# Mixers' second half reordered with other PSUM banks, and upward products with both halves of the activations in one moving operand

## The reference, cut to what matters

```
for l in range(2):
    h = rmsnorm(x, norm_mix_g[l])
    uv, z, xbc, dt_raw, c_q, c_kv, k_rope = split_cols(h @ w_in[l])
    y_a = gmlp_mixer(uv, ...)        # gelu, spatial gate: u * (W_s v + b)
    y_b = ssd_mixer(z, xbc, ...)     # state space mixer
    y_c = mla_mixer(c_q, c_kv, ...)  # 6 heads of causal attention, chunks of 128
    x = x + concat(y_a, y_b, y_c) @ w_out[l]
    x = x + square(relu(rmsnorm(x, norm_mlp_g[l]) @ w1)) @ w2     # 1024 -> 4096 -> 1024
return rmsnorm(x, final_norm_g)
```

## Time and profile before

| | |
|---|---|
| median of 3 runs | 1304.95 us (1301.78 to 1305.06; all: 1304.95, 1305.06, 1301.78) |
| profiled execution | 1302.27 us, span 1300.5 us, mean granted clock 0.998 |
| PE busy | 1258.7 us (97%), 8024 matmuls |
| DVE busy | 870.8 us (67%) |
| ACT busy | 705.1 us (54%) |
| mixers and feed-forward part, layer d0 | about 690 to 818 us and 818 to 997 us of the span |
| the same, layer d1 | about 1000 to 1114 us and 1114 to 1293 us |

### The profile page before, as it was taken

One profiled execution on the slowest core, in us unless ns is written; L12 is line 12 of the kernel. 1 busy time (PEld: TensorE's weight loads), 2 busy tenths in 40 slices (PEclk: granted clock), 3 DMA queues, 4 the chain that ended last, 5 costly groups with the idle time before them and its releaser, 6 DMA issues.

```text
span 1300.5 us, 20111 instructions
## 1 busy us (share of the span) xinstructions
PE 1258.7 (97%) x8024; PEld 1100.9 (85%) x8024; DVE 870.8 (67%) x1570; ACT 705.1 (54%) x1029; POOL 2.4 (0%) x8
## 2 busy tenths in 40 slices
PE   8999999999999999999999999999999999999996
PEld 7997787878888787877998987999998987999895
DVE  6677996684664756548557997655547897665545
ACT  5634577454467666575536675634444576544442
POOL 0000000000000000000000000000000000000000
PEclk9999999999999999999999999999999999999999
DMA  9454532444643335233353544465655544456660
GB/s 273 148 170 136 162 115 81 162 162 162 209 148 130 128 105 170 84 130 106 114 168 100 176 140 132 160 196 181 207 163 150 150 162 119 148 188 193 195 210 33
DMA packets 147058, 197.28 MB, mean 152 GB/s; under 512 B 4732, under 2 KB 102294, under 8 KB 146966
## 3 DMA queue, kind: packets, MB, share of 16 engines
q1 hardware_dynamic: 146838, 195.96, 47.0%
q0 software_dynamic: 128, 0.04, 0.0%
HBM read 194.94 MB, written 1.05 MB: 151 GB/s over the span
## 4 chain that ended last, share of the span: by engine, by line
PE 78%; DVE 12%; ACT 5%; issue 4%; SPq 1%; DMA 0%; DVEq 0%; ACTq 0%
PE bank L481 22%; PE bank L483 22%; PE bank L482 22%; PE bank L569 4%; DVE w_lo L2144 3%; DVE stat L2164 2%; PE bank L1064 1%; PE bank L778 1%; PE bank L682 1%; PE bank L1101 1%; ACT w_hi L1578 1%; DVE stat L2161 1%; DVE arena L2158 1%; PE bank L926 1%; DVE stat L2158 1%
## 5 line engine op out<-in xcount | busy, mean ns | idle before, releaser
L2144 DVE TENSOR_TENSOR w_lo<-w_raw,w_hi 128x2048 fp32r<-128x2048 f32 (+5 forms) x190 | 413.8, 2183 | 139.2 <-ACT w_hi L1578 136.9
L1578 ACT ACTIVATE w_hi<-w_raw 128x2048 fp32r<-128x2048 f32 (+5 forms) x190 | 346.2, 1828 | 282.6 <-PE bank L483 273.1
L481 PE MATMUL bank<-h_hi,w_hi 128*128 128x256 f32 x976 | 279.2, 286 | 4.3 <-DVE w_lo L2144 2.4
L482 PE MATMUL bank<-h_lo,w_hi 128*128 128x256 f32 x976 | 276.1, 283 | 0.0
L483 PE MATMUL bank<-h_hi,w_lo 128*128 128x256 f32 x976 | 276.0, 283 | 0.0
L481 PE MATMUL bank<-w_hi,r_hi 128*128 128x512 f32 (+3 forms) x536 | 207.3, 387 | 3.9 <-DVE r_lo L2843 2.0
L482 PE MATMUL bank<-w_lo,r_hi 128*128 128x512 f32 (+3 forms) x536 | 204.1, 381 | 0.0
L483 PE MATMUL bank<-w_hi,r_lo 128*128 128x512 f32 (+3 forms) x536 | 204.1, 381 | 0.0
L481 PEld LDWEIGHTS bank<-h_hi,w_hi 128*128 128x128 f32 x976 | 187.0, 192 | 12.0 <-issue 9.3
L482 PEld LDWEIGHTS bank<-h_lo,w_hi 128*128 128x128 f32 x976 | 187.1, 192 | 0.5
L483 PEld LDWEIGHTS bank<-h_hi,w_lo 128*128 128x128 f32 x976 | 187.0, 192 | 0.0
(11 more groups left out here) (301 smaller groups left out, 1368.9 us busy)
## 6 DMA issues: line engine op xcount, KB each, us to landing
w_raw<-in_mlp_w SPq DMA_DIRECT2D x64, 1024.0 KB, 5.4
w_raw<-in_w_out SPq DMA_DIRECT2D x24, 1024.0 KB, 5.1
w_raw<-in_w_in_c SPq DMA_DIRECT2D x48, 512.0 KB, 4.6
w_raw<-in_w_in_c SPq DMA_DIRECT2D x18, 1024.0 KB, 5.1
w_raw<-in_w_in_a SPq DMA_DIRECT2D x12, 1024.0 KB, 7.4
w_raw<-in_w_in_b SPq DMA_DIRECT2D x12, 1024.0 KB, 5.1
w_raw<-in_w_in SPq DMA_DIRECT2D x8, 1024.0 KB, 5.2
w_raw<-in_w_out SPq DMA_DIRECT2D x8, 512.0 KB, 3.7
```

Source lines behind the costliest of these rows:

```text
L481: nc.tensor.matmul(o, lhs[0], rhs[0], start=start, stop=False)
L482: nc.tensor.matmul(o, lhs[0], rhs[1], start=False, stop=False)
L1578: nc.scalar.activation(w_hi[:, u % SPLIT_SLOTS, 0:kts * n], w_raw[:, u % RAW_SLOTS, 0:kts * n], ACT.Copy).then_inc(w_rounded.sem, w_rounde ...
L2144: v.tensor_tensor(w_lo[:, s, 0:m], w_raw[:, u % RAW_SLOTS, 0:m], w_hi[:, s, 0:m].bitcast(F32), ALU.subtract)\
```

## The change

Mixers' second half:
- KT_BANK goes from (3, 0, 3) to (3, 0, 0), HEAD_BANK from (3, 6) to (4, 6), and the six heads' scores from the banks 4, 5, 4, 5, 4, 5 to 4, 5, 6, 3, 4, 5.
- PE: turn_mixer comes before turn_heads(2).
- ACT: head_tiles(2) comes after the mixer's high parts; the rounding for ("uv", 1), which is that of the unit mix_out(0, 1), goes from ahead of pair_exp(1) to behind pair_turned(1); that for ("t", 3), the unit mix_out(1, 1), from ahead of the "co" 0 copy to behind pair_turned(2).
- DVE: pair_max(0) comes after spatial_norm and the mixer's low parts; pair_max(2) before pair_normal(1); the split of the unit mix_out(1, 0), weights(("uv", 1), 2), after pair_normal(1).

Feed-forward part, upward products:
- h_hi and h_lo become two halves of one tensor h_both, and the eight banks one tensor.
- For each tile m and k-tile, one matmul with w_hi stationary takes [h_hi | h_lo], 512 columns, into a whole bank, and one with w_lo stationary takes h_hi, 256 columns, into the bank's first half. A unit uses two banks, 2u and 2u + 1.
- ACT copies the second halves of both banks to SBUF (in place of Relu). DVE adds them to the first halves, then computes max(f, 0) * f in one instruction. ACT copies that into r_hi (in place of Square), DVE subtracts as before.

```diff
-        QT_BANK, KT_BANK, ... HEAD_BANK, ... = (7, 6, 7), (3, 0, 3), 7, (1, 2), (3, 6), (6, 7)
+        QT_BANK, KT_BANK, ... HEAD_BANK, ... = (7, 6, 7), (3, 0, 0), 7, (1, 2), (4, 6), (6, 7)
+        MLA_SCORE_BANK = (4, 5, 6, 3, 4, 5)
...
                 turn_heads(1)
+                turn_mixer()
                 turn_heads(2)
-                turn_mixer()
                 scores(1)
...
                 def up(e):
                     for u in range(2):
-                        feature_major((L, "up", e, u), (2 * e + u) % 4, ...)
+                        key = (L, "up", e, u)
+                        for m in range(2):
+                            if 2 * u + m in left:
+                                pe.wait_ge(*left[2 * u + m])
+                            left[2 * u + m] = up_summed.after(key)
...
+                            for m in range(2):
+                                o = bank[2 * u + m]
+                                for k in range(k0, k0 + step):
+                                    hi, lo = [a[:, k, m * P:(m + 1) * P] for a in w]
+                                    nc.tensor.matmul(o, hi, h_both[:, :, k, :], start=k == 0, stop=False)
+                                    i = nc.tensor.matmul(o[:, 0:S], lo, h_hi[:, k, :], start=False, stop=k == KT - 1)
...
                 head_tiles(1)
-                head_tiles(2)
                 act.wait_ge(product_done.sem, product_done.at((L, "bt", 0)))
...
+                head_tiles(2)
                 pair_exp(0)
...
-                round_weights((L, "uv", 1))
                 pair_exp(1)
                 pair_turned(0)
                 pair_exp(2)
                 pair_turned(1)
-                round_weights((L, "t", 3))
+                round_weights((L, "uv", 1))
...
                 pair_turned(2)
+                round_weights((L, "t", 3))
...
-                        nc.scalar.activation(relu, bank[t][:, :], ACT.Relu).then_inc(act_read.sem, act_read.next((L, "up", e, u)))
+                        nc.scalar.activation(low, up_sums(e, u, 1), ACT.Copy).then_inc(up_low.sem, up_low.next(key))
...
+                        act.wait_ge(up_square.sem, up_square.at(key))
-                        nc.scalar.activation(flat2(r_hi[:, t0:t0 + 2, :]), relu, ACT.Square)...
+                        nc.scalar.activation(flat2(r_hi[:, t0:t0 + 2, :]), split_t[:, u, :], ACT.Copy)...
...
                 mixer_norm()
-                pair_max(0)
                 spatial_norm()
...
+                pair_max(0)
                 spatial_gate()
                 pair_max(1)
                 split_lo((L, "at"), ...)
                 pair_normal(0)
+                pair_max(2)
+                pair_normal(1)
                 weights((L, "uv", 1), 2)
-                pair_normal(1)
-                pair_max(2)
                 pair_normal(2)
...
-                        tt(f, relu, relu, MUL)
+                        v.tensor_tensor(f..., up_sums(e, u, 0), low..., ADD).then_inc(up_summed.sem, up_summed.next(key))
+                        dve.wait_ge(up_summed.sem, up_summed.at(key))
+                        v.scalar_tensor_tensor(f, f, 0.0, f, ALU.max, MUL).then_inc(up_square.sem, up_square.next(key))
```

More of the change, by code:

```diff
@@ L160, in build @@
         w_lo = sb("w_lo", [P, SPLIT_SLOTS, UNIT], F32R)
-        h_hi = sb("h_hi", [P, KT, S], F32R)
-        h_lo = sb("h_lo", [P, KT, S], F32R)
+        h_both = sb("h_both", [P, 2, KT, S], F32R)
+        h_hi, h_lo = h_both[:, 0, :, :], h_both[:, 1, :, :]
         r_hi = sb("r_hi", [P, YT, S], F32R)
@@ L183, in build, with up_sums @@
         arena = sb("arena", [P, ARENA])
-        bank = [ctx.enter_context(nc.psum_tensor(f"bank{i}", [P, 512], F32)) for i in range(8)]
+        banks_all = ctx.enter_context(nc.psum_tensor("bank", [P, 8, 512], F32))
+        bank = [banks_all[:, i, :] for i in range(8)]
+        def up_sums(e, u, part):
+            at = 2 * u
+            return banks_all[:, at:at + 2, part * S:(part + 1) * S]
         def K(name):
@@ L253, in build @@
         square_hi = Steps("square_hi")
+        up_low = Steps("up_low")
+        up_summed = Steps("up_summed")
+        up_square = Steps("up_square")
         latent_normal = Steps("latent_normal")
@@ L388, in build @@
         XS_BANK, CB_BANK, WST_BANK, UV_BANK, ST_BANK, YD_BANK, YO_BANK = (4, 5), 0, 6, (1, 2), 4, (5, 0), 4
-        QT_BANK, KT_BANK, GATING_BANK, MIXER_BANK, HEAD_BANK, MLA_TURN_BANK = (7, 6, 7), (3, 0, 3), 7, (1, 2), (3, 6), (6, 7)
+        QT_BANK, KT_BANK, GATING_BANK, MIXER_BANK, HEAD_BANK, MLA_TURN_BANK = (7, 6, 7), (3, 0, 0), 7, (1, 2), (4, 6), (6, 7)
+        MLA_SCORE_BANK = (4, 5, 6, 3, 4, 5)
         block = ctx.enter_context(nc.Block())
@@ L1363, in scores @@
                     for h in (2 * p, 2 * p + 1):
-                        o = taken(4 + h % 2, dve_read, (L, "s", h))
+                        o = taken(MLA_SCORE_BANK[h], dve_read, (L, "s", h))
                         for b in range(NB):
@@ L1476, in up @@
                     for u in range(2):
[L1477 to L1480, removed]
+                        key = (L, "up", e, u)
[3 more added lines that the diff above has]
+                            left[2 * u + m] = up_summed.after(key)
+                        at, w = unit(rows_of(A["mlp_w1_2"][l], 0, KT, (2 * e + u) * 256, 256))
+                        step = 2 if e + u == 0 else KT
+                        for k0 in range(0, KT, step):
+                            if e + u == 0:
+                                pe.wait_ge(h_ready.sem, h_ready.at(((L, "mlp"), k0 // 2)))
+                            for m in range(2):
[4 more added lines that the diff above has]
+                                    i = nc.tensor.matmul(o[:, 0:S], lo, h_hi[:, k, :], start=False, stop=k == KT - 1)
+                            if e + u + k0 == 0:
+                                stream_tiles((L, "mlp"), (L, "wo"), 1)
+                        i.then_inc(product_done.sem, product_done.next(key))
+                        unit_done[at] = key
                 def down(e):
@@ L2114, in _ @@
                     for u in range(2):
[L2115 to L2120, removed]
-                        nc.scalar.activation(relu, bank[t][:, :], ACT.Relu).then_inc(act_read.sem, act_read.next((L, "up", e, u)))
-                        act.wait_ge(act_read.sem, act_read.at((L, "up", e, u)))
+                        key = (L, "up", e, u)
+                        round_weights(key)
+                        act.wait_ge(product_done.sem, product_done.at(key))
+                        if e >= 1:
+                            act.wait_ge(up_summed.sem, up_summed.at((L, "up", e - 1, u)))
+                        low = masked[:, u, :].rearrange("p (m s) -> p m s", m=2)
+                        nc.scalar.activation(low, up_sums(e, u, 1), ACT.Copy).then_inc(up_low.sem, up_low.next(key))
                         if e >= 2:
                             act.wait_ge(product_done.sem, product_done.at(down_done[L, e - 2]))
+                        act.wait_ge(up_square.sem, up_square.at(key))
                         t0 = 4 * (e % 2) + 2 * u
-                        nc.scalar.activation(flat2(r_hi[:, t0:t0 + 2, :]), relu, ACT.Square).then_inc(square_hi.sem, square_hi.next((L, "up", e, u)))
+                        nc.scalar.activation(flat2(r_hi[:, t0:t0 + 2, :]), split_t[:, u, :], ACT.Copy).then_inc(square_hi.sem, square_hi.next(key))
             round_weights(("d1", "dn", 1, 1))
@@ L2852, in pair_max @@
                         product((L, "s", h), 0)
-                        o = bank[4 + h % 2]
+                        o = bank[MLA_SCORE_BANK[h]]
                         for b, (c0, c1) in enumerate(((0, P), (P, P + S))):
@@ L2974, in _ @@
                     for u in range(2):
-                        weights((L, "up", e, u))
-                        dve.wait_ge(square_hi.sem, square_hi.at((L, "up", e, u)))
-                        relu, f = masked[:, u, :], split_t[:, u, :]
-                        tt(f, relu, relu, MUL)
+                        key = (L, "up", e, u)
+                        f = split_t[:, u, :]
+                        low = masked[:, u, :]
+                        weights(key)
+                        dve.wait_ge(up_low.sem, up_low.at(key))
+                        v.tensor_tensor(f.rearrange("p (m s) -> p m s", m=2), up_sums(e, u, 0), low.rearrange("p (m s) -> p m s", m=2), ADD)\
+                            .then_inc(up_summed.sem, up_summed.next(key))
+                        dve.wait_ge(up_summed.sem, up_summed.at(key))
+                        v.scalar_tensor_tensor(f, f, 0.0, f, ALU.max, MUL).then_inc(up_square.sem, up_square.next(key))
+                        dve.wait_ge(up_square.sem, up_square.at(key))
+                        dve.wait_ge(square_hi.sem, square_hi.at(key))
                         t0 = 4 * (e % 2) + 2 * u
```

(2 more changed lines are left out.)

## The result

The changed kernel takes 1296.82 us (median of 5 runs, 1295.11 to 1297.46), the kernel before 1303.87 us in the same comparison (1301.78 to 1305.06). The ratio is 0.9946, 95% interval [0.9934, 0.9958]: faster by 7.0 us (5.5 to 8.6). The profiled executions took 1295.20 and 1302.27 us, with spans of 1293.4 and 1300.5. The forecast was 1294.0, in a range of 1290 to 1301, and a gain of 9.3 us. Sign and range held; the gain was three quarters of the forecast, and its two parts were both off, one down and one up.

The account below looks back on a forecast made before the run. PE's own instruction stream was taken to bound the feed-forward part, a chain of engines the mixers' second half. Gains of 6.7 + 2.6 = 9.3 us took the profiled 1302.27 to 1293.0; the median was put at 1294.0, range 1290 to 1301.

Parts of the forecast that it names:

- Upward products: Feed-forward part: one fixed matmul cost saved per tile and k-tile, 6.8 us over both layers, taken as 6.7 us.
- 226.7 + 120.0 = 346.7 ns: Feed-forward upward products: one 512-column plus one 256-column matmul per tile and k-tile, in place of 360 ns.
- the seam: Upward products: wide matmul's moving operand in two stretches 8 KB apart; 0 to 5.5 us, taken as 0; rival chance 0.12.
- The fixed part: Upward products: 13.3 ns of each matmul's time belong to the instruction and not to its columns.
- The slower rival: Upward products: weight load behind each narrow matmul stands bare by 41 ns, 21.0 us in all, giving 1314.0 us; chance 0.06.
- The rival in which the mixers give nothing: Mixers' second half: PE's wait at mix_out(1, 0) takes all the gain back, giving 1295.6 us; chance 0.13.
- the new wait: Mixers' second half: PE waits 0.8 us for DVE's weight split before mix_out(1, 0), replacing part of the gain.
- DVE and ACT: Feed-forward part: DVE 0.8 us later per unit, low part ending at 5.3 us; PE waits for neither split nor banks.
- Mixers up to the new wait: Mixers' second half: spatial() starts at 779.6 instead of 780.69, its 1.2 us wait falls to about 0.2.
- Mixers' gain: Mixers' second half: 1.3 us a layer, 2.6 us in all, with the heads' values moved to bank 4.
- - 1.02: Mixers' second half: removed bank 3 wait at 797.30, subtracted to put PE's start at 795.98.
- The sum: Whole kernel: 6.7 us from upward products plus 2.6 us from mixers, a gain of 9.3 us.

Follow-up runs that it names:

- the two other orders measured: Changed kernel with a tile's eight wide (512-column) matmuls ahead of its eight narrow (256-column) ones: 1294.37 us; with wide, wide, narrow, narrow: 1294.0 us.
- with 384 columns over the load: Kernel with the moving operand in one piece, its narrow matmul widened from 256 to 384 columns, in turn with the wide one: 1325.34 us (one execution).

## Why the prediction was right or wrong

- **Upward products, the failed term.** The step "226.7 + 120.0 = 346.7 ns" took the two spacings from runs of equal widths and added them for a strict alternation that no row had. Measured 353 ns: the edit gives 3.0 us, not 6.7. The prediction held against this that no gap shows where wide gives way to narrow (849.03, 849.26, 849.37), but one such place, read to 0.01 us, can't show 6 ns. The unknown I named for this step was the seam, bounded at 5.5 us; it costs nothing (1297.16 against 1296.82 us). The order of the same instructions was the unknown I did not see; the two other orders measured are 2.5 and 2.8 us faster than the change's by the medians, and 1.3 and 1.5 us in d1's feed-forward stretch alone.
- **The fixed part** of 13.3 ns per matmul is right: with equal widths side by side a unit takes 5.56 to 5.59 us, against 5.55 in the sum, and 7.25 us with 512 columns throughout. The 2.5 ns of the Trainium skill ("TensorE: Matmul & The Clock Gate", Back-to-back issue gap), which the page gives for a matmul by itself, would have made the units 5.72 us (5.76 less 16 x 2.5 ns).
- **The slower rival**, a load of weights that stands bare behind each narrow matmul, is refuted: in the kernel with the operand in one piece the start behind a narrow one comes after 0.117 us, no later than the sum's 0.120, and with 384 columns over the load the cost is still there.
- **The rival in which the mixers give nothing** is refuted: they give 1.6 us a layer alone, and the new wait ends within 0.1 us of where the sum had it.
- **DVE and ACT.** Right. The low part ends at 5.3 us after the wake-up (819.27 to 824.58), there is no PE wait for w_lo or for the sum in the feed-forward part. In order of time, DVE of the changed kernel has the sum, the square and the low part, and DVE's split where it computes the row factors starts 7.6 us after the wake-up of 858.47, as the sum had it within 0.1 us (861.03 to 867.75 before, 6.7, and 0.8 more):

```profile
855.25 0.69 DVE L3005 TENSOR_TENSOR split_t<-bank,masked 128x512 f32<-128x512 f32 x1 [3.83 <-ACT masked L2146]
855.97 0.69 DVE L3008 SCALAR_TENSOR_TENSOR split_t<-split_t 128x512 f32<-128x512 f32 x1
857.50 0.69 DVE L3012 TENSOR_TENSOR r_lo<-split_t,r_hi 128x512 fp32r<-128x512 f32 x1 [0.83 <-ACT r_hi L2151]
...
866.04 4.49 DVE L2169 TENSOR_TENSOR w_lo<-w_raw,w_hi 128x2048 fp32r<-128x2048 f32 x2
```

- **Mixers up to the new wait.** Right to 0.1 us, and for the reason given. With the 0.36 us added by which the changed kernel runs ahead at scores(0): spatial at 779.55 (forecast 779.6), PE at mix_out(1, 0) at 791.33 (forecast 791.3). Of the wait before spatial 0.26 us are left by the starts (scores(1) at 777.62 to spatial at 779.19 is 1.57, and scores(0) takes 1.31), where the forecast had about 0.2.
- **Mixers' gain.** Behind it PE came to 795.71 on the same clock, where I had 795.98: 1.6 us a layer in place of 1.3. The step "- 1.02" took the idle time of the earlier trace rows for the price of the wait. By the starts it was 1.27: the third pair's transposes start at 794.72 and the next matmul at 795.35 after, 0.63 apart; before, 0.63 after 795.40 is 796.03, and it started at 797.30. The new wait is under-read alike, 0.62 for 0.87.
- **The sum** came out as near as it did partly by luck: one term was too high by 3.7 us and the other too low by 0.6, and 0.9 us of the profiled 7.1 came from parts I had not counted. Of these 0.36 lie before d0 and are scatter, and 0.37 in the first half of d1's mixers, which the upward edit shortens by a path I have not followed.

## What to carry to other kernels

Price a reordered or merged stream from rows in the same order, not from the sum of two uniform streams; where 512 and 256 columns have to be mixed, try two of a width in a row. Price a wait by the distance between starts, with and without it, and not by the idle time of the row. When a bank is given to another product, look up who reads its present contents last: here the bank paid only with the order that freed it.

## What the runs showed of the hardware

Matmuls of two widths in strict turn, each with its own load of weights, cost 6 ns a pair more than the sum of their spacings: 353 ns a pair for 512 and 256 columns (347 by the sum), 406 for 512 and 384 (400, and 413 in a layer's first units), and nothing for 512 and 512, all at a granted clock of 1.00 (2.4 GHz). Two by two, 512 and 256 take 348. A moving operand in two stretches 8 KB apart runs as one in a single piece (1296.82 and 1297.16 us).
